# Residual sums of a decoder layer made by accumulating transfers instead of VectorE

## The chip, the cores and the metric

One core of a Trainium2 chip runs the whole kernel. The metric is the device time of one execution in microseconds, as the median of several. The core has five instruction streams: TensorE (PE), VectorE (DVE), ScalarE (ACT), GpSimd (POOL) and SyncE (SP). They run on their own and meet at semaphores. SP and POOL issue transfers, which 16 DMA engines carry out.

## The reference, cut to what matters

One layer of a hybrid decoder for 512 prompt tokens and 64 sample tokens, 2048 wide: mixer, cross-attention into a memory, squared-ReLU MLP, each behind an RMSNorm and followed by one ("sandwich"). The change touches the two places where a sub-layer's output is normalized, added to x, and x is normalized for the next sub-layer:

```python
x = x + rmsnorm(mix @ w_out, g_mix_post)
x = x + rmsnorm(cross_attn(rmsnorm(x, g_mem_pre), mem_k, mem_v, w_mem_q, w_mem_o), g_mem_post)
x = x + rmsnorm(sq_relu_mlp(rmsnorm(x, g_mlp_pre), w_up, w_down), g_mlp_post)
```

with `rmsnorm(x, g) = x * rsqrt(mean(x*x) + eps) * g` over the 2048 features. The two places are the first `+` with the norm `g_mem_pre` behind it, and the second `+` with `g_mlp_pre` behind it.

## The kernel before

Activations lie transposed: 128 features on the partitions, 16 chunks (`KC`) of features, 576 tokens along each row. `xT` is x, `yT` the sub-layer's output, both 128 x 16 x 576 float32, so one chunk is 288 KB. Matrix products keep float32 accuracy by splitting both operands in a high and a low part: three products hi*hi, hi*lo, lo*hi per tile (`parts`, line 1987, six matmuls of 288 columns for one chunk and one stripe of weights). A stripe of weights goes raw by a transfer (`w_load`, L508), high part by ScalarE (`hi`, L833 and `hi_halves`, L1028), low part by VectorE (`lo`, L1239 and `lo_halves`, L1681).

The residual stage runs twice, k = 0 behind the mixer and k = 1 behind the cross-attention. Per chunk c:

- VectorE, `residual` (L1711): `scale` multiplies yT by the row factors `n_rt` (named rstd_b in the profile, L1694; chunk 0 in halves from PSUM, L1718) and counts in `n_t`; `add` multiplies by the gain and adds into xT (L1701) and counts in `n_x`; `low` makes `act_lo` = xT * gain - act_hi (L1708) and counts in `n_lo`. The order is scale(c+2), low(c), add(c+2).
- ScalarE, `residual` (L1056): waits for `n_x`, makes `act_hi` (L1068) and the square of x in `n_sq` (L1073, named z_out), the latter only when TensorE has used the buffer (`n_used`).
- TensorE, `first_tiles` (L2365): for each chunk `col_sums` over the squares (L2353), then the six matmuls of chunk c for the first stripe. From chunk `behind` on (4 for k = 0, 6 for k = 1), each step also does chunk c - behind of the second stripe, ahead of the first stripe's. What remains of the second stripe follows, then the row factors are spread (L2361).
- SyncE: in k = 0 it waits for all 16 additions before it loads the cross-attention's caches into memory that yT holds (L594 on). In k = 1 it stores xT to HBM, four chunks at a time, each time the four are added (L618 to L621); that copy is read back near the end (L818).
- GpSimd has nothing to do in either stage.

The norm's factor for the next sub-layer isn't applied to the operands but to the product afterwards, so TensorE can start on chunk 0 before the sum over all chunks is known.

Of the kernel before, what the change touches and what calls it, by code (L numbers as in the profile page):

```python
# [14 lines left out]
F32 = mybir.dt.float32  # L15
# [148 lines left out]
def program(nc, x_prompt, x_sample, mem_prompt, state_ret, cache_k, cache_v, cache_mk, cache_mv, pages,  # L164
# [5 lines left out]
    with ctx:  # L170
# [3 lines left out]
        def sem(name):  # L174
            return ctx.enter_context(nc.semaphore(name))
# [304 lines left out]
        n_x = sem("n_x")  # L480
# [30 lines left out]
        def _(sp):  # L511
# [82 lines left out]
            sp.wait_ge(n_x, KC)  # L594
# [54 lines left out]
        def _(pool):  # L649
# [173 lines left out]
        def _(act):  # L823
# [232 lines left out]
            def residual(k, g_pre, stripe, tile):  # L1056
# [6 lines left out]
                with act.Fori(0, KC // 2) as i:  # L1063
                    for b in range(2):
                        act.wait_ge(n_x, i * 2 + (k * KC + b + 1))
                        act.sem_inc(s_idle, 1)
                        x = xT[:, bass.ds(2 * i + b, 1), :].rearrange("p a t -> p (a t)")
                        nc.scalar.activation(act_hi[:, bass.ds(2 * i + b, 1), :].rearrange("p a t -> p (a t)"), x,  # L1068
                                             ACT.Copy, scale=gT[:, bass.ds(2 * i + (g_pre + b), 1)]).then_inc(n_hi, 1)

                        act.wait_ge(n_used, i * 2 + (k * KC + b + 1))
                        act.sem_inc(s_idle, 1)
                        nc.scalar.activation(n_sq[b][:], x, ACT.Square).then_inc(n_xsq, 1)  # L1073
# [154 lines left out]
        def _(dve):  # L1228
# [1439 lines left out]
```

## Time and profile before

| | us |
|---|---|
| median of 3 runs | 3084.23 |
| lowest, highest | 3084.04, 3086.8 |
| the profiled execution | 3081.77 |
| its span | 3080.1 |
| TensorE busy | 3013.3 (98%) |
| VectorE busy | 1278.9 (42%) |
| ScalarE busy | 767.5 (25%) |
| GpSimd busy | 149.6 (5%) |
| mean granted TensorE clock | 0.992 |

"Busy" is the time in which an engine has at least one instruction under way. Times inside the profile count from the span's start. The two residual stages are short stretches of it: k = 0 from about 1211 to 1258 us, k = 1 from about 1393 to 1441 us. A timeline lists instructions with their start and duration; where one is followed by [0.69 <-DVE act_lo], its engine stood idle that long before it, until that instruction released it. Instructions overlap at their ends, so the cost of one in a row of many is the distance between starts.

### The profile page before, as it was taken

To read this page: it belongs to the slowest core of one execution; us is meant where nothing else is said; L and a number is where in the kernel's file an instruction comes from. 1 tells how busy PE (TensorE), PEld (TensorE's weight loads), DVE (VectorE), ACT (ScalarE), POOL (GpSimd) and SP (SyncE) were. 2 spreads that over 40 slices of the span, in tenths; PEclk is the share of its full clock that TensorE was granted. 3 is DMA by queue.
4 is the path that set the end of the run, shared out by engine and by line. 5 is a ranking of instruction groups with operands and counts; after the bars stand their busy time and mean duration, and the time that the engine had idled before them with its cause. 6 is when DMAs were issued, how large, how long until landed. Compare 5 with 4: busy or idle time off the path is not lost.

```text
span 3080.1 us, 48385 instructions
## 1 busy us (share of the span) xinstructions
PE 3013.3 (98%) x20106; PEld 2749.1 (89%) x20106; DVE 1278.9 (42%) x1839; ACT 767.5 (25%) x862; POOL 149.6 (5%) x254
## 2 busy tenths in 40 slices
PE   7999999999999999998999999999999999999998
PEld 6899999999899998777989889899898898998976
DVE  6544245455554445557333333323323333233235
ACT  4311123322322233434212112112121121121222
POOL 0000002312211000000000000000000000000000
PEclk8999999999999999999999999999999999999999
DMA  5433435545656453423222222222222222222242
GB/s 181 161 105 105 149 115 168 166 137 171 211 160 229 148 191 106 138 69 117 92 80 75 94 72 85 88 76 87 82 82 82 82 82 82 82 82 82 82 152 80
DMA packets 366166, 356.19 MB, mean 116 GB/s; under 512 B 9446, under 2 KB 296412, under 8 KB 363900
## 3 DMA queue, kind: packets, MB, share of 16 engines
q1 hardware_dynamic: 344696, 269.18, 28.5%
q0 software_dynamic: 21152, 85.70, 8.2%
q8 instruction: 62, 1.02, 0.1%
q14 instruction: 28, 0.23, 0.0%
q10 hardware_dynamic: 228, 0.06, 0.0%
HBM read 306.67 MB, written 48.23 MB: 115 GB/s over the span
## 4 chain that ended last, share of the span: by engine, by line
PE 91%; issue 3%; DVE 2%; DMA 2%; ACT 1%; POOL 1%; DVEq 0%; POOLq 0%; ACTq 0%
PE gemm L1987 55%; PE aux L2581 7%; PE aux L2582 7%; PE aux L2583 7%; PE gemm L2586 2%; PE gemm L2585 2%; PE aux L2093 1%; PE gemm L2070 1%; PE gemm L2016 1%; PE aux L1987 1%; DMA w_raw<-in_w_in 1%; PE aux L2133 1%; PE aux L2149 1%; DMA g_row<-in_norm_mlp_post 1%; DMA d_vp<-in_cache_diff_v 0%
## 5 line engine op out<-in xcount | busy, mean ns | idle before, releaser
L1987 PE MATMUL gemm<-act_hi,w_hi 128*128 128x288 f32 x4480 | 980.4, 300 | 6.3 <-DVE yT L1662 3.6
L1987 PE MATMUL gemm<-act_lo,w_hi 128*128 128x288 f32 x4480 | 960.2, 296 | 0.0
L1987 PE MATMUL gemm<-act_hi,w_lo 128*128 128x288 f32 x4480 | 959.8, 296 | 0.0
L1987 PEld LDWEIGHTS gemm<-act_hi,w_hi 128*128 128x128 f32 x4480 | 720.7, 189 | 37.9 <-issue 23.9
L1987 PEld LDWEIGHTS gemm<-act_hi,w_lo 128*128 128x128 f32 x4480 | 722.9, 189 | 0.0
L1987 PEld LDWEIGHTS gemm<-act_lo,w_hi 128*128 128x128 f32 x4480 | 722.8, 189 | 0.0
L1239 DVE TENSOR_TENSOR w_lo<-w_raw,w_hi 128x2048 fp32r<-128x2048 f32 x214 | 489.9, 2290 | 467.0 <-ACT w_hi L1186 325.9
L2581 PE MATMUL aux<-w_hi,u_hi 128*128 128x512 f32 x1024 | 399.7, 390 | 6.3 <-DVE w_lo L1239 6.3
L2582 PE MATMUL aux<-w_hi,u_lo 128*128 128x512 f32 x1024 | 399.0, 390 | 0.0
L2583 PE MATMUL aux<-w_lo,u_hi 128*128 128x512 f32 x1024 | 398.9, 390 | 0.0
L1186 ACT ACTIVATE w_hi<-w_raw 128x2048 fp32r<-128x2048 f32 x63 | 120.6, 1915 | 539.4 <-PE aux L2583 539.4
L833 ACT ACTIVATE w_hi<-w_raw 128x2048 fp32r<-128x2048 f32 x89 | 170.3, 1914 | 326.6 <-PE gemm L1987 256.6
L2581 PEld LDWEIGHTS aux<-w_hi,u_hi 128*128 128x128 f32 x1024 | 192.6, 188 | 49.9 <-DVE w_lo L1239 6.7
L2583 PEld LDWEIGHTS aux<-w_lo,u_hi 128*128 128x128 f32 x1024 | 192.7, 188 | 40.5
L2582 PEld LDWEIGHTS aux<-w_hi,u_lo 128*128 128x128 f32 x1024 | 192.7, 188 | 40.0
L1863 DVE SCALAR_TENSOR_TENSOR z_out<-gemm,rstd_b 128x288 f32<-128x288 f32 x126 | 51.8, 453 | 399.5 <-PE gemm L1987 397.3
L1175 ACT ACTIVATE z_out<-z_out 128x576 f32<-128x576 f32 x64 | 43.9, 686 | 603.4 <-DVE z_out L1863 603.4
L1170 ACT ACTIVATE w_hi<-w_raw 128x2048 fp32r<-128x2048 f32 x62 | 118.0, 1904 | 75.7 <-PE aux L2583 75.7
L1885 DVE TENSOR_TENSOR y_tok<-y_tok,aux 128x512 f32 x96 | 65.9, 687 | 114.2 <-PE aux L2583 114.2
L2586 PE MATMUL gemm<-w_lo,u_hi 128*64 128x512 f32 x256 | 101.4, 396 | 0.0
L2585 PE MATMUL gemm<-w_hi,u_hi 128*128 128x512 f32 x256 | 99.7, 390 | 0.0
L1868 DVE TENSOR_TENSOR u_lo<-z_out,u_hi 128x512 f32 (+1 forms) x64 | 44.3, 693 | 115.0 <-ACT u_hi L1177 115.0
(344 smaller groups left out, 2043.7 us busy)
## 6 DMA issues: line engine op xcount, KB each, us to landing
w_raw<-in_w_mlp_up SPq DMA_DIRECT2D x64, 1024.0 KB, 6.5
w_raw<-in_w_mlp_down SPq DMA_DIRECT2D x64, 1024.0 KB, 5.0
w_raw<-in_w_in SPq DMA_DIRECT2D x56, 1024.0 KB, 5.7
w_raw<-in_w_out SPq DMA_DIRECT2D x16, 1024.0 KB, 6.3
z_scratch<-z_out SPq DMA_DIRECT2D x56, 288.0 KB, 2.1
r_zin<-z_scratch POOLq DMA_DIRECT2D x8, 1152.0 KB, 6.7
d_z<-z_scratch POOLq DMA_DIRECT2D x12, 576.0 KB, 7.3
xin<-in_x_prompt POOLq DMA_DIRECT2D x6, 1024.0 KB, 6.8
```

What stands on the lines that cost most here:

```text
L833: nc.scalar.activation(w_hi[b][:], w_raw[b][:], ACT.Copy).then_inc(s_whi, 1)
L1170: nc.scalar.activation(w_hi[(b + 1) % 2][:], w_raw[(b + 1) % 2][:], ACT.Copy).then_inc(s_whi, 1)
L1186: nc.scalar.activation(w_hi[(b + 1) % 2][:], w_raw[(b + 1) % 2][:], ACT.Copy).then_inc(s_whi, 1)
L1239: V.tensor_tensor(w_lo[b][:], w_raw[b][:], w_hi[b][:].bitcast(F32), ALU.subtract).then_inc(s_wlo, 1)
L1863: ins = V.scalar_tensor_tensor(out=u_t[:, cols], in0=(G if b else bank)[2 * b + half][:, 0:TH], scalar=0.0, in1=rstd_b[:, cols], op0=ALU.m ...
L1885: ins = V.tensor_tensor(y, y, y_bank[t][:], ALU.add)
L1987: ins = M(out[half][:, 0:TH], w[b][:, cols], x[:, k, half * TH:(half + 1) * TH], start=first and n == 0, stop=last and n == 2)
L2581: M(A[t][:], hi, w_hi[b][:, cols], start=c == 0, stop=False)
L2582: M(A[t][:], lo, w_hi[b][:, cols], start=False, stop=False)
L2583: ins = M(A[t][:], hi, w_lo[b][:, cols], start=False, stop=c == FC - 1)
L2585: M(G[2][:], u_hi[:, c, TP:T + TS], w_hi[b][:, cols], start=c == 0, stop=False, skip_group_check=True)
L2586: ins = M(G[2][0:TS, :], u_hi[:, c, TP:T], w_lo[b][:, cols], start=False, stop=c == FC - 1, skip_group_check=True)
```

## The change

VectorE no longer adds. Its scaling multiplies by the row factor and by the gain in one instruction (`scalar_tensor_tensor`). GpSimd issues, for each chunk, a transfer from yT to xT that adds into the destination (`accum_op=ALU.add`), as soon as the chunk is scaled. Up to four are in flight: chunk c waits until that of chunk c - 4 has landed. Each of four semaphores `n_xd` counts the landings of every fourth chunk; they take the place of `n_x`, and `x_added` waits for them on ScalarE, VectorE and SyncE. `low(c)` runs four chunks behind the scaling instead of two. The loops over chunks on VectorE, ScalarE and SyncE are written out instead of being loops of the engine.

```diff
+        def x_added(eng, k, c):
+
+            eng.wait_ge(n_xd[c % 4], 16 * (4 * k + c // 4 + 1))
...
-            sp.wait_ge(n_x, KC)
+            for c in range(KC - 4, KC):
+                x_added(sp, 0, c)
...
-            with sp.Fori(0, KC // 4) as i:
-                sp.wait_ge(n_x, 4 * i + (KC + 4))
-                sp.sem_inc(s_idle, 1)
-                sp.dma_start(x_d[:, bass.ds(4 * i, 4), :], xT[:, bass.ds(4 * i, 4), :]).then_inc(s_spill, 16)
+            for i in range(KC // 4):
+                for c in range(4 * i, 4 * i + 4):
+                    x_added(sp, 1, c)
+                sp.dma_start(x_d[:, 4 * i:4 * i + 4, :], xT[:, 4 * i:4 * i + 4, :]).then_inc(s_spill, 16)
...
+            for k in range(2):
+                for c in range(KC):
+                    pool.wait_ge(n_t, k * KC + c + 1)
+                    if k or c >= 4:
+                        pool.wait_ge(n_xd[c % 4], 16 * (4 * k + c // 4))
+                    pool.dma_start(xT[:, c, :], yT[:, c, :], accum_op=ALU.add).then_inc(n_xd[c % 4], 16)
...
-                with act.Fori(0, KC // 2) as i:
-                    for b in range(2):
-                        act.wait_ge(n_x, i * 2 + (k * KC + b + 1))
...
+                for c in range(KC):
+                    x_added(act, k, c)
+                    nc.scalar.activation(act_hi[:, c, :], xT[:, c, :], ACT.Copy, scale=gT[:, g_pre + c:g_pre + c + 1]).then_inc(n_hi, 1)
+                    act.wait_ge(n_used, k * KC + c + 1)
+                    nc.scalar.activation(n_sq[c % 2][:], xT[:, c, :], ACT.Square).then_inc(n_xsq, 1)
...
-            def scale(c):
-                y = flat(yT[:, bass.ds(c, 1), :])
-                V.tensor_tensor(y, y, n_rt[:], ALU.mult).then_inc(n_t, 1)
-
-            def add(k, c, g_post):
-
-                at = bass.ds(c, 1)
-                x, y = flat(xT[:, at, :]), flat(yT[:, at, :])
-                dve.wait_ge(n_t, c + (k * KC + 1))
-                V.scalar_tensor_tensor(out=x, in0=y, scalar=gT[:, bass.ds(c + g_post, 1)], in1=x,
-                                       op0=ALU.mult, op1=ALU.add).then_inc(n_x, 1)
+            def scale(c, g_post):
+                y = yT[:, c, :]
+                V.scalar_tensor_tensor(out=y, in0=y, scalar=gT[:, g_post + c:g_post + c + 1], in1=n_rt[:],
+                                       op0=ALU.mult, op1=ALU.mult).then_inc(n_t, 1)
...
-                add(k, 0, g_post)
                 dve.wait_ge(n_bcs, 4 * k + 2)
-                scale(1)
-                add(k, 1, g_post)
-                with dve.Fori(0, KC - 2) as c:
-                    scale(c + 2)
+                for c in range(1, KC):
+                    scale(c, g_post)
+                    if c >= 4:
+                        low(k, c - 4, g_pre)
+                for c in range(KC - 4, KC):
                     low(k, c, g_pre)
-                    add(k, c + 2, g_post)
-                low(k, KC - 2, g_pre)
-                low(k, KC - 1, g_pre)
```

VectorE's stream at the start of the stage k = 0, before. The rows from the branch on are the loop, which runs 14 times:

```order
L1718 TENSOR_TENSOR yT<-yT,aux 128x288 [waits n_bc]
L1718 TENSOR_TENSOR yT<-yT,aux 128x288
L1701 SCALAR_TENSOR_TENSOR xT<-yT,gT,xT 128x576 [waits n_t]
L1694 TENSOR_TENSOR yT<-yT,rstd_b 128x576 [waits n_bcs]
L1701 SCALAR_TENSOR_TENSOR xT<-yT,gT,xT 128x576 [waits n_t]
L1724 UNCONDITIONAL_BRANCH
L1724 ISA
L1694 TENSOR_TENSOR yT<-yT,rstd_b 128x576
L1706 REGISTER_ALU
L1708 ISA [waits n_hi,n_x]
L1708 ISA
L1708 SCALAR_TENSOR_TENSOR act_lo<-xT,gT,act_hi 128x576
```

The same place now (line numbers of the changed kernel; n_xd0 to n_xd3 are the landing counts):

```order
L1716 SCALAR_TENSOR_TENSOR yT<-yT,gT,aux 128x288 [waits n_bc]
L1716 SCALAR_TENSOR_TENSOR yT<-yT,gT,aux 128x288
L1700 SCALAR_TENSOR_TENSOR yT<-yT,gT,rstd_b 128x576 [waits n_bcs]
L1700 SCALAR_TENSOR_TENSOR yT<-yT,gT,rstd_b 128x576 x3
L1706 SCALAR_TENSOR_TENSOR act_lo<-xT,gT,act_hi 128x576 [waits n_hi,n_xd0]
L1700 SCALAR_TENSOR_TENSOR yT<-yT,gT,rstd_b 128x576
L1706 SCALAR_TENSOR_TENSOR act_lo<-xT,gT,act_hi 128x576 [waits n_hi,n_xd1]
L1700 SCALAR_TENSOR_TENSOR yT<-yT,gT,rstd_b 128x576
```

Four scalings stand ahead of the first low part where one scaling and two additions stood, and nothing of VectorE writes xT any more.

GpSimd's stream behind its last loads of the mixer, before:

```order
L799 DMA yT<-y_scratch 128x2x576 [waits s_zst1,s_zst0,s_xt]
L799 DMA yT<-y_scratch 128x2x576 [waits s_zst1,s_zst0] x3
L818 DMA act_hi<-x_scratch 128x9216 [waits s_tile,s_spill]
L819 DMA g_row<-in_norm_mlp_post 128x2048
L170 UNCONDITIONAL_BRANCH
```

And now, cut to its first rows:

```order
L804 DMA yT<-y_scratch 128x2x576 [waits s_zst1,s_zst0,s_xt]
L804 DMA yT<-y_scratch 128x2x576 [waits s_zst1,s_zst0] x3
L826 DMA xT<-yT 128x576 [waits n_t] x4
L826 DMA xT<-yT 128x576 [waits n_xd0,n_t]
L826 DMA xT<-yT 128x576 [waits n_xd1,n_t]
L826 DMA xT<-yT 128x576 [waits n_xd2,n_t]
```

32 accumulating transfers (16 per stage) stand between the loads of yT and the load of x_scratch near the end of the kernel.

## Rows read from the trace of the kernel before

**Rows 1.** The page's list of busy us, share, instructions.

```profile
PE 3013.3 (98%) x20106; PEld 2749.1 (89%) x20106; DVE 1278.9 (42%) x1839; ACT 767.5 (25%) x862; POOL 149.6 (5%) x254
```

**Rows 2.** Chain that ended last, 1205 to 1300: start us, us, what.

```profile
1229.45 1.79 PE gemm L1987 x12
1231.62 1.78 PE gemm L1987 x12
...
1255.07 1.93 ACT w_hi L833
1257.02 2.30 DVE w_lo L1239
```

**Rows 3.** Timeline of VectorE, k = 0: start us, us, instruction, idle before.

```profile
1217.61 0.82 DVE L1701 SCALAR_TENSOR_TENSOR xT<-yT,gT,xT 128x576 f32<-128x576 f32 x1
...
1220.55 0.81 DVE L1708 SCALAR_TENSOR_TENSOR act_lo<-xT,gT,act_hi  x1
1221.28 0.81 DVE L1701 SCALAR_TENSOR_TENSOR xT<-yT,gT,xT  x1
1222.01 0.75 DVE L1694 TENSOR_TENSOR yT<-yT,rstd_b 128x576 f32 x1
1222.68 0.81 DVE L1708 SCALAR_TENSOR_TENSOR act_lo<-xT,gT,act_hi  x1
```

**Rows 4.** Timeline of VectorE, k = 1, the first addition.

```profile
1399.41 0.82 DVE L1701 SCALAR_TENSOR_TENSOR xT<-yT,gT,xT 128x576 f32<-128x576 f32 x1
```

**Rows 5.** Timeline of TensorE, k = 0: chunk 0's sums, chunks 0 to 3.

```profile
1220.26 0.71 PE L2353 MATMUL aux<-z_out,ones 128*32 128x144 f32 x8 [4.31 <-ACT z_out L1073]
1221.42 0.85 PE L1987 MATMUL gemm<-act_hi,w_hi 128*128 128x288 f32 x2 [0.46 <-DVE act_lo L1708]
...
1223.80 0.85 PE L1987 MATMUL gemm<-act_hi,w_hi 128*128 128x288 f32 x2
...
1226.17 0.85 PE L1987 MATMUL gemm<-act_hi,w_hi 128*128 128x288 f32 x2
...
1228.01 0.53 PE L1987 MATMUL gemm<-act_hi,w_hi 128*128 128x288 f32 x2
```

**Rows 6.** Stretches: length, busy us, granted clock, DMA share, GB/s.

```profile
1218.00:1222.00 4.00, 1.29 (x10) 0.81 (x11) 3.96 (x6) 3.02 (x6) 0.00 (x0) 0.50 0.96 262
1400.00:1404.00 4.00, 1.49 (x11) 1.02 (x12) 3.96 (x7) 2.82 (x5) 0.00 (x0) 0.50 0.89 244
1407.00:1409.00 2.00, 2.00 (x16) 1.14 (x15) 2.00 (x4) 1.31 (x3) 0.00 (x0) 0.72 1.01 424
953.00:957.00 4.00, 4.00 (x32) 3.44 (x31) 2.84 (x7) 2.64 (x3) 0.75 (x2) 1.00 1.08 382
```

**Rows 7.** Timeline of TensorE, k = 1: chunks 2 to 5, then sums of 6.

```profile
1407.97 0.59 PE L1987 MATMUL gemm<-act_hi,w_hi 128*128 128x288 f32 x2
...
1409.60 0.54 PE L1987 MATMUL gemm<-act_hi,w_hi 128*128 128x288 f32 x2
...
1411.73 0.53 PE L1987 MATMUL gemm<-act_hi,w_hi 128*128 128x288 f32 x2 [0.69 <-DVE act_lo L1708]
...
1413.86 0.53 PE L1987 MATMUL gemm<-act_hi,w_hi 128*128 128x288 f32 x2 [0.69 <-DVE act_lo L1708]
...
1414.85 0.45 PE L2353 MATMUL aux<-z_out,ones 128*32 128x144 f32 x8
```

**Rows 8.** Groups of instructions, the additions: busy us, mean ns, idle before.

```profile
L1701 DVE SCALAR_TENSOR_TENSOR xT<-yT,gT,xT (+1 forms) x32 | 26.3, 821 | 0.1
```

**Rows 9.** Line 788, GpSimd's four stores of 288 KB, 839.8 to 952.6.

```profile
L788 POOL DMA_DIRECT2D mix_hi_scratch<-r_yhi x4: 559/566/572, 839.8 to 952.6; - x4
...
DMA to landing us min/median/max: 3.3/3.8/4.6
```

**Rows 10.** Timeline of ScalarE, k = 0: one chunk.

```profile
1222.40 0.78 ACT L1068 ACTIVATE act_hi<-xT,gT  x1 [0.77 <-DVE xT L1701]
1223.09 0.67 ACT L1073 ACTIVATE z_out<-xT 128x576 f32 x1
```

**Rows 11.** Timeline of SyncE: cache load in k = 0, stores in k = 1.

```profile
1249.78 0.38 SPq L595 DMA_DIRECT2D c_mk<-out  x1
...
1406.26 25.87 SPq L621 DMA_DIRECT2D x_scratch<-xT  x4
```

**Rows 12.** Timeline of all engines, 1158 to 1166: GpSimd's issues and VectorE.

```profile
1160.11 2.86 POOL L799 DMA_DIRECT2D yT<-y_scratch  x4 [21.51 <-PE aux L2093]
...
1160.28 0.76 DVE L1672 TENSOR_TENSOR n_acc<-n_acc,z_out 128x576 f32<-128x576 f32 x1 [0.75 <-ACT z_out L1042]
```

More of the change, by code:

```diff
@@ L479, in program @@
         n_even = sem("n_even")
-        n_x = sem("n_x")
+        n_xd = [sem(f"n_xd{b}") for b in range(4)]
         n_xsq = sem("n_xsq")
@@ L1062, in residual @@
                 spread(n_y_bc)
-                with act.Fori(0, KC // 2) as i:
-                    for b in range(2):
-                        act.wait_ge(n_x, i * 2 + (k * KC + b + 1))
[L1066 to L1073, printed above, removed]
+                for c in range(KC):
[3 more added lines that the diff above has]
+                    nc.scalar.activation(n_sq[c % 2][:], xT[:, c, :], ACT.Square).then_inc(n_xsq, 1)
                 act.wait_ge(n_used, (k + 1) * KC + 2)
@@ L1690, in flat @@
                 return a.rearrange("p a t -> p (a t)")
-            def scale(c):
-                y = flat(yT[:, bass.ds(c, 1), :])
-                V.tensor_tensor(y, y, n_rt[:], ALU.mult).then_inc(n_t, 1)
-            def add(k, c, g_post):
-                at = bass.ds(c, 1)
-                x, y = flat(xT[:, at, :]), flat(yT[:, at, :])
-                dve.wait_ge(n_t, c + (k * KC + 1))
-                V.scalar_tensor_tensor(out=x, in0=y, scalar=gT[:, bass.ds(c + g_post, 1)], in1=x,
-                                       op0=ALU.mult, op1=ALU.add).then_inc(n_x, 1)
+            def scale(c, g_post):
+                y = yT[:, c, :]
+                V.scalar_tensor_tensor(out=y, in0=y, scalar=gT[:, g_post + c:g_post + c + 1], in1=n_rt[:],
+                                       op0=ALU.mult, op1=ALU.mult).then_inc(n_t, 1)
             def low(k, c, g_pre):
-                at = bass.ds(c, 1)
-                dve.wait_ge(n_x, c + (k * KC + 1))
+                x_added(dve, k, c)
                 dve.wait_ge(n_hi, c + (k * KC + 1))
-                V.scalar_tensor_tensor(out=flat(act_lo[:, at, :]), in0=flat(xT[:, at, :]), scalar=gT[:, bass.ds(c + g_pre, 1)],
-                                       in1=flat(act_hi[:, at, :]).bitcast(F32), op0=ALU.mult, op1=ALU.subtract).then_inc(n_lo, 1)
+                V.scalar_tensor_tensor(out=act_lo[:, c, :], in0=xT[:, c, :], scalar=gT[:, g_pre + c:g_pre + c + 1],
+                                       in1=act_hi[:, c, :].bitcast(F32), op0=ALU.mult, op1=ALU.subtract).then_inc(n_lo, 1)
             def residual(k, g_post, g_pre, stripe):
@@ L1717, in residual @@
                     y = yT[:, 0, half * TH:(half + 1) * TH]
-                    ins = V.tensor_tensor(y, y, n_y_bc[half], ALU.mult)
+                    ins = V.scalar_tensor_tensor(out=y, in0=y, scalar=gT[:, g_post:g_post + 1], in1=n_y_bc[half],
+                                                 op0=ALU.mult, op1=ALU.mult)
                 ins.then_inc(n_t, 1)
-                add(k, 0, g_post)
                 dve.wait_ge(n_bcs, 4 * k + 2)
-                scale(1)
-                add(k, 1, g_post)
-                with dve.Fori(0, KC - 2) as c:
-                    scale(c + 2)
+                for c in range(1, KC):
[3 more added lines that the diff above has]
+                for c in range(KC - 4, KC):
                     low(k, c, g_pre)
-                    add(k, c + 2, g_post)
-                low(k, KC - 2, g_pre)
-                low(k, KC - 1, g_pre)
                 recip(2 * k + 2)
```

## The prediction

> **What bounds the kernel now.** The page first: TensorE is busy 98% of the span, VectorE 42%, GpSimd 5% [rows 1]. So a change to VectorE's work can only matter where TensorE waits for it, and I looked for these places. The edited functions run twice, in the two residual stages: k = 0 (from 1217 us) and k = 1 (from 1399 us). In the chain of waits of k = 0 [rows 2] the reader sees VectorE and ScalarE only up to the first chunk; from 1229.45 it is TensorE alone, about 1.78 us of matmuls every 2.16 us, until the weights of the third stripe (ACT and DVE, 1255 to 1259).
>
> I call T the end of the scaling of chunk 0: 1217.61 in k = 0, 1399.41 in k = 1, where the first addition starts [rows 3, 4]. VectorE's period per chunk is 2.13 us (scale, low part, addition: 1220.55 to 1222.68 between low parts) [rows 3]. TensorE in k = 0 starts chunk 0 at T+3.81. Chunks 0 and 1 take 2.38 us each at the low clock (granted 0.50, the level of 1.2 GHz), the next 1.84, and chunk 4's two-chunk step begins 1.44 after that [rows 2, 5, 6]. The first two are longer than VectorE's 2.13, which puts VectorE far enough ahead for the next two, and from chunk 4 on a step has two chunks of matmuls and 2.16 us. So in k = 0 TensorE is its own bound from chunk 0 on. In k = 1 two-chunk steps start only at chunk 6; there the rows show TensorE waiting 0.69 us for act_lo twice, with steps of 2.13 where 1.37 would do (the step from 1413.86 to the matmuls of chunk 6: its col_sums at 1414.85, 0.38 of them) [rows 7]. **That is all that a faster VectorE can give back**: 0.76 twice, plus 0.2 on the step before (1.63 against 1.43), 1.7 us.
>
> **What is removed and what it gives.** 32 additions of 0.82 us, 26.3 us of VectorE time [rows 8]. The gain multiply moves into the scaling, which stays one instruction (0.75 us, at most 0.82 as a scalar_tensor_tensor) [rows 3]. VectorE's period falls to about 1.5 us, below TensorE's 2.16 and near its 1.37. Gain: 1.7 us in k = 1, nothing in k = 0. The loops are written out, which removes register work and adds instructions to fetch; both lie beside VectorE's new slack, and I cost them at nothing (a late fetch would show as a gap of VectorE or ScalarE without a releaser).
>
> **What is added: latency ahead of chunk 0.** The sum of chunk 0 took 0.82 us on VectorE. Now it is a transfer: GpSimd sees n_t, issues, 16 engines read xT and yT, add, write, and only then ScalarE may start. No transfer of the kernel before accumulates, so I bound it. The nearest rows are GpSimd's stores of one 288 KB chunk: 3.3, 3.8, 4.6 us to landing (min, median, max) [rows 9]. The max is that of the last one, issued at 952.63, and from 953 to 957 the DMA engines were at a share of 1.08 [rows 6]. That is the case here too: w_load of the next stripe moves its 1 MB in these four microseconds, share 0.96 and 0.89 [rows 6]. An accumulation reads a second operand. A plain chunk costs 0.7 us of all 16 engines (294,912 B at some 420 GB/s, read off the first x_scratch store, which moves at 1407 to 1409 [rows 6, 11]), so I add 0.7: **L = 5.3 us**, bounds 3.3 (quiet engines, the second read for nothing) and 6.0 (4.6 plus 1.4, the second read at half speed beside the load).
>
> From the landing, ScalarE starts 0.3 later (addition's end 1222.09, act_hi 1222.40), its square starts 0.69 later and takes 0.67, col_sums follows 0.13 behind and takes 0.64 before the chunk's matmuls [rows 3, 5, 10]. That is 2.43: the sums, not the low part, now come last (low part: 0.3 + 0.78 + 0.06 + 0.82 = 1.96). The four scalings that now stand before low(0) end at T+3.7, ahead of T+L, and cost nothing unless L falls below about 2.1. Chunk 0 starts at T + 5.3 + 2.43 = T+7.73, against T+3.81: **+3.9 us in each stage**, 7.8 in all. Nothing covers it: TensorE has no other matmuls in its queue there.
>
> **What is added: the rate of the transfers.** Call D the engines' time for one accumulation; I take twice a plain chunk, 1.4 us, since two operands are read; bounds 0.7 (a plain chunk) and 2.8 (as if the add took as long again as both reads; no row is nearer). The sums of chunks land at T+5.3, T+8.0 (the load still has 1.3 us of work), then every 1.4. Chunk c's col_sums can start 1.8 after its landing. In k = 0 chunk 1 is needed at T+9.5 and ready at T+9.8: +0.3; all later ones are ahead of TensorE, whose steps are 2.16. So k = 0 is **+4.2**.
> In k = 1 SyncE also stores x_scratch, 1.18 MB after every fourth chunk, 2.8 us of all engines by the same rate [rows 6, 11], now against the accumulations. Landings: T+5.3, 8.0, 9.4, 10.8, then sharing with the first store 13.0, 15.8, 18.0, 19.4, and so on up to 36.5. TensorE would want col_sums of chunk 5 at T+16.6 and can have it at 17.6, of chunk 6 at 18.9 and can have it at 19.8; from there the two go side by side (chunk 9: 26.3 wanted, 26.1 ready; chunk 15: 39.2 and 38.3). Chunk 6 started at T+15.44 before (1414.85) [rows 7], so k = 1 is 19.8 - 15.44 = **+4.4** (that is 3.9 + 0.3 + 1.9 of waits - 1.7 of gain).
> Behind the waits: GpSimd has nothing else queued (its last issues before are those at 1160.11 [rows 12], and the x_back load stands behind the MLP). VectorE's low(c-4) holds up scale(c+1), with the lead that TensorE's pace gives it. SyncE's cache loads waited for the last addition (1249.78) and are free at about T+28, earlier; its x_scratch stores are needed by ScalarE's first square of the MLP, behind all 16 chunks [rows 11]. Neither is on the path.
>
> **Sum.** 4.2 + 4.4 = +8.6 us. The profiled execution has 3081.77 us, 1.7 around its span of 3080.1: it would become 3090.4. The median of three is 2.5 us above it, 3084.23, so single runs differ by a good part of the effect; the same 8.6 us on the median give 3092.8 us.
>
> **Two rules of the Trainium skill.** A GpSimd-issued transfer needs GpSimd to write descriptors. The trace: four issues at 1160.11 took 2.86 us, 0.71 each, while VectorE ran the n_acc sum with two SBUF inputs at 1160.28 [rows 12]; nothing shows that one was held up. The Trainium skill, "SBUF — State Buffer", section "Who interferes with whom", says that a VectorE instruction with two SBUF inputs contends with GpSimd instructions that read SBUF, not with those that only write it, and that its 2-port modes lock GpSimd out of writing descriptors. By its first half nothing changes; a lock is the third rival below.
> The Trainium skill, "Collectives: The Full Stack", section "The bandwidth ceiling: the fold count and why AG ≠ RS ≠ AR", says that an add in a DMA engine costs its second read and nothing for the add, measured as 1.93 times a copy. By it D would be 0.7 x 1.93 = 1.35 (an estimate from that page), and the sum would be the same within 1 us; no row of this trace shows an add.
>
> **Rivals.** (a) *The transfers set the pace.* If D is 2.8, chunk 15 lands at about T+49 in k = 0 and, with the three stores, T+58 in k = 1, and TensorE has it 1.8 later, where it had it at T+35.1 (eleven steps of 2.16 behind chunk 4's) and T+34.9 (nine behind chunk 6's) [rows 2, 7]: +16 and +25, 3125 us. It decides from D = 1.9 (k = 0) or 1.5 (k = 1). For it: no row shows an accumulation, and k = 1 has no slack at 1.4. Against: it needs the add itself to cost time. At D = 2.1 the sum is about +18. 0.20.
> (b) *Not slower.* If the transfer finds a gap and the second read is hidden, L is 3.3: chunk 0 starts at T+5.73, +1.9 per stage, and with D under 1.2 no waits follow: 3.8 - 1.7 = +2.1, 3086.3 us. For it: small stores landed in 3.3 us. Against: the weight load is in flight at that very time in both stages. It decides below L = 5.2 where no waits follow, below about 4 with waits of my size. A little below it: TensorE finds more chunks ready when it restarts and gets its clock back sooner, worth at most 2 us per stage (two chunks at 2.38 that could take 1.37), which ends near 3082; a gain over 0.2% needs that and more. 0.24, of which 0.04 for such a gain.
> (c) *VectorE starves GpSimd.* VectorE runs without a gap from T to T+3.7; if descriptors wait for that, L is 9.0 and each stage loses 3.7 more: 8.6 + 7.4 = +16, 3100 us. The even issues at 1160.11 speak against it [rows 12]. 0.06.
> The forecast (latency in both stages, between 3088 and 3099): 0.50.
>
> **How the numbers follow.** The likeliest case gives 3092.8. The range reaches down past (b)'s 3086.3 to 3085.5 and up to 3114, which is D of about 2.5 (+30), and takes in (c); above it lies a part of (a), below it little. About 0.2%, 6 us, is what a measurement can tell from no change. Slower by more: (c), (a), and most of the forecast (from 3090.4 up): 0.06 + 0.20 + 0.38 = 0.64. Same: the rest of the forecast and most of (b): 0.12 + 0.20 = 0.32. Faster: 0.04.
>
> **What would show it.** In the profile of the changed kernel: landing of the first accumulation of each stage 5.3 us after issue (right), under 4 (b), 9 or more (c). TensorE's first chunk at T+7.7. In the timeline of k = 0, steps of 2.16 us from chunk 4 to 15; longer ones with waits for act_hi or a DMA mean (a). ScalarE's wait before act_hi should be for a DMA. The mean clock should be as now, 0.99. The stage k = 1 should no longer show steps of 2.13 at chunks 3 and 4 if landings keep up. The forecast is wrong if an accumulation costs the engines other than 1.4 us, or if chunk 0 is not late.

## The result and the profile after

| | before | after |
|---|---|---|
| median of 8 runs each, us | 3084.86 | 3094.35 |
| lowest, highest | 3082.98, 3086.8 | 3091.38, 3097.73 |
| span of the profiled execution | 3080.1 | 3092.0 |
| mean granted TensorE clock | 0.992 | 0.989 |

After to before is 1.0032, with an interval of 1.0023 to 1.0041: 9.5 us slower, where 8.6 were forecast.

The page's busy list of the changed kernel, the answer to [rows 1]: VectorE has lost 20 us of work and GpSimd has gained 27, and TensorE, the engine that counts, has not changed.

```profile
PE 3014.4 (97%) x20106; PEld 2749.9 (89%) x20106; DVE 1258.9 (41%) x1807; ACT 767.3 (25%) x862; POOL 176.3 (6%) x286
```

The timeline of the stage k = 0 after the change, all engines (start, duration, engine, instruction, idle before it and what ended that), answering to [rows 3], [rows 5] and [rows 10]:

```profile
1218.42 0.93 DVE L1716 SCALAR_TENSOR_TENSOR yT<-yT,gT,aux 128x288 f32<-128x288 f32 x2
1218.66 0.37 SPq L512 DMA_DIRECT2D w_raw<-in_w_mem_q  x1
...
1219.67 0.95 POOL L826 DMA_DIRECT2D xT<-yT  x1 [55.06 <-DVE yT L1716]
1220.13 3.00 DVE L1700 SCALAR_TENSOR_TENSOR yT<-yT,gT,rstd_b 128x576 f32<-128x576 f32 x4 [0.78 <-ACT rstd_b L1048]
1221.25 2.58 POOL L826 DMA_DIRECT2D xT<-yT  x3 [0.64 <-DVE yT L1700]
1225.28 0.78 ACT L1077 ACTIVATE act_hi<-xT,gT 128x576 fp32r<-128x576 f32 x1 [5.19 <-DMA xT<-yT]
...
1226.16 0.82 DVE L1706 SCALAR_TENSOR_TENSOR act_lo<-xT,gT,act_hi 128x576 fp32r<-128x576 f32 x1 [3.03 <-ACT act_hi L1077]
1226.69 0.78 ACT L1077 ACTIVATE act_hi<-xT,gT 128x576 fp32r<-128x576 f32 x1
...
1226.78 0.71 PE L2349 MATMUL aux<-z_out,ones 128*32 128x144 f32 x8 [9.18 <-ACT z_out L1079]
...
1227.41 0.85 PE L1983 MATMUL gemm<-act_hi,w_hi 128*128 128x288 f32 x2
```

T, the end of the scaling of chunk 0, is 1218.42 + 0.93 = 1219.35. GpSimd issues at once, and ScalarE, idle for 5.19 us until the DMA, starts act_hi at T+5.9 (before: T+1.2). Chunk 0's matmuls start at T+8.1. TensorE stood idle 9.18 us ahead of them, where it stood 4.31 before [rows 5].

The same in k = 1, where T is 1404.07 + 0.93 = 1405.00, with TensorE's three later waits for chunks 6, 10 and 15:

```profile
1404.07 0.93 DVE L1716 SCALAR_TENSOR_TENSOR yT<-yT,gT,aux 128x288 f32<-128x288 f32 x2
1404.17 0.37 SPq L512 DMA_DIRECT2D w_raw<-in_w_mlp_up  x1
...
1412.12 0.77 ACT L1077 ACTIVATE act_hi<-xT,gT 128x576 fp32r<-128x576 f32 x1 [6.38 <-DMA xT<-yT]
...
1413.61 0.71 PE L2349 MATMUL aux<-z_out,ones 128*32 128x144 f32 x8 [10.41 <-ACT z_out L1079]
...
1414.25 0.85 PE L1983 MATMUL gemm<-act_hi,w_hi 128*128 128x288 f32 x2
...
1424.87 0.45 PE L2349 MATMUL aux<-z_out,ones 128*32 128x144 f32 x8 [0.16 <-ACT z_out L1079]
...
1433.86 0.45 PE L2349 MATMUL aux<-z_out,ones 128*32 128x144 f32 x8 [0.29 <-ACT z_out L1079]
...
1445.72 0.45 PE L2349 MATMUL aux<-z_out,ones 128*32 128x144 f32 x8 [0.99 <-ACT z_out L1079]
```

The col_sums of chunk 15 are the last sign of a stage. They start at 1258.38 and 1445.72, T+39.0 and T+40.7. Before the change they started at T+35.2 and T+34.9 (T at 1217.58 and 1399.37), as these two rows of TensorE's timeline of the kernel before show:

```profile
1252.74 0.45 PE L2353 MATMUL aux<-z_out,ones 128*32 128x144 f32 x8
...
1434.27 0.45 PE L2353 MATMUL aux<-z_out,ones 128*32 128x144 f32 x8
```

So k = 0 is 3.9 us longer and k = 1 5.8 us. T itself comes 0.1 later in each stage, since the scaling of chunk 0 with the gain takes 0.93 us instead of 0.81. That makes 9.9 us, where the medians differ by 9.5; the profiled spans differ by 11.9, of which the other 2.0 lie ahead of k = 0 (1.6) and behind k = 1 (0.5), where nothing was edited.

What the DMA engines carried, in stretches of the changed kernel (length, busy us by engine, granted clock, DMA share, GB/s), beside [rows 6]:

```profile
1219.00:1225.00 6.00, 0.00 (x0) 0.00 (x0) 3.35 (x5) 0.71 (x2) 3.53 (x4) 0.50 0.95 236
1236.00:1242.00 6.00, 6.00 (x58) 4.83 (x57) 4.91 (x8) 3.72 (x6) 2.98 (x4) 1.00 1.08 187
...
1405.00:1409.00 4.00, 0.00 (x0) 0.00 (x0) 3.00 (x4) 0.71 (x2) 2.85 (x4) 0.69 0.68 175
...
1409.00:1440.00 31.00, 25.94 (x223) 20.07 (x224) 19.01 (x25) 19.03 (x28) 10.74 (x13) 0.82 1.09 262
```

From 1236 to 1242 only accumulations were under way: full engines, yet 187 GB/s, so the 294,912 B of one chunk take 1.58 us. In k = 1 the engines are full for 31 us on end. And the transfers, line 826 (issue durations in ns, then us to landing):

```profile
L826 POOL DMA_DIRECT2D xT<-yT x32: 832/848/1237, 1219.7 to 1435.2; - x32
...
DMA to landing us min/median/max: 4.2/6.3/9.1
```

### The profile page after: what moved, and what is told of

Read it like the earlier page. It is cut to its first block, busy times and chain, and to the rows that moved or that the text cites. A ratio compares the mean times of both kernels' runs of the same rounds, so it can differ in the third digit from the quotient of the medians.

```text
span 3092.0 us, 47978 instructions
## 1 busy us (share of the span) xinstructions
PE 3014.4 (97%) x20106; PEld 2749.9 (89%) x20106; DVE 1258.9 (41%) x1807; ACT 767.3 (25%) x862; POOL 176.3 (6%) x286
## 4 chain that ended last, share of the span: by engine, by line
PE 88%; issue 7%; DMA 3%; DVE 1%; POOL 1%; ACT 0%; DVEq 0%; POOLq 0%; ACTq 0%
PE gemm L1983 53%; PE aux L2577 7%; PE aux L2578 7%; PE aux L2579 7%; PE gemm L2582 2%; PE gemm L2581 2%; PE aux L2089 1%; PE gemm L2066 1%; DMA xT<-yT 1%; PE gemm L2012 1%; DMA w_raw<-in_w_in 1%; PE aux L2129 1%; PE aux L2145 1%; DMA g_row<-in_norm_mlp_post 1%; DMA d_vp<-in_cache_diff_v 0%
## 5 line engine op out<-in xcount | busy, mean ns | idle before, releaser
L1983 PEld LDWEIGHTS gemm<-act_hi,w_hi 128*128 128x128 f32 x4480 | 720.9, 189 | 35.3 <-issue 25.7
```

The source lines that it names most:

```text
L1983: ins = M(out[half][:, 0:TH], w[b][:, cols], x[:, k, half * TH:(half + 1) * TH], start=first and n == 0, stop=last and n == 2)
```

## The experiments

One table first; each experiment's reading follows. "Chunk 0" and "chunk 15" are the starts of their col_sums from T in us, k = 0 / k = 1; the next column is how much later chunk 15 is than before, both stages summed. The ratio is to the kernel before as it ran beside that kernel (medians of 3084.86 for the changed kernel, 3085.36 for e_load and e_dve4, 3085.28 for the others). Kernels with one run have no ratio.

| kernel | chunk 0 | chunk 15 | stages | median us (runs) | ratio |
|---|---|---|---|---|---|
| before | 2.7 / 2.7 | 35.2 / 34.9 | 0 | 3084.86 (8) | 1 |
| after | 7.4 / 8.6 | 39.0 / 40.7 | +9.7 | 3094.35 (8) | 1.0032 [1.0023, 1.0041] |
| e_load | 5.4 / 5.3 | 39.6 / 42.7 | +12.3 | 3099.83 (4) | 1.0049 [1.0032, 1.0066] |
| e_copy | 7.0 / 8.4 | 38.1 / 40.0 | +8.0 | 3088.39 (1) | |
| e_store | 7.3 / 8.8 | 39.4 / 37.9 | +7.3 | 3087.31 (1) | |
| e_dve4 | 2.3 / 2.3 | 36.4 / 38.5 | +4.9 | 3092.93 (8) | 1.0024 [1.0013, 1.0035] |
| e_quiet | 5.4 / 5.3 | 36.9 / 35.7 | +2.5 | 3087.68 (10) | 1.0009 [0.9999, 1.0018] |
| e_quiet4 | 2.3 / 2.3 | 36.7 / 35.5 | +2.1 | 3092.35 (10) | 1.0020 [1.0010, 1.0029] |
| e_quiet4b | 2.3 / 2.3 | 36.4 / 35.5 | +1.8 | 3087.44 (1) | |
| e_dve16 | 2.3 / 2.3 | 35.1 / 34.9 | 0.0 | 3086.55 (10) | 1.0005 [0.9996, 1.0014] |
| e_qcopy | 4.2 / 4.2 | 36.0 / 33.7 | -0.3 | 3085.78 (1) | |
| e_qsp | 4.0 / 4.0 | 35.3 / 33.2 | -1.6 | 3081.27 (1) | |

Single executions scatter by some 4 us around a median, in part outside the stages: between the last sign of k = 0 and T of k = 1 the profiled e_dve4 and e_quiet4 took 1.7 and 1.9 us longer than the kernel before (granted clocks 0.97 against 0.98), e_load 0.9, the others at most 0.2. So a single time tells little here and the stage columns more. They too are read from one execution each, and one thing moves them by chance: when the clock rises. From the col_sums of chunk 0 to those of chunk 4, TensorE took 8.28 us in k = 1 of the changed kernel, 9.39 in that of e_copy and 6.91 in that of e_store, none with a wait; in k = 0 the kernels without a wait lie between 7.35 (e_copy) and 8.34 (e_store). A difference of about 1 us in a stage is therefore no finding by itself. "Chunk 0" is free of this.

**e_load.** Is L long because of the weights? The load of the fourth stripe, which moves 1 MB beside the first accumulations, is held until chunk 3 has landed.

```diff
             for n in range(MH):
                 sp.wait_ge(s_wlo, S_MQ + n - 1)
+                if n == 3:
+                    x_added(sp, 0, 3)
                 w_load(sp, None, n % 2, mq_v[:, :, n * P:(n + 1) * P], KC)
```

(The same with `x_added(sp, 1, 3)` in the MLP's load loop.)

> The changed kernel, but SyncE's 1 MB load of the fourth stripe of weights waits until chunk 3 has been added, in both stages, so that it no longer shares the engines with the first accumulations. Theory A (the loss is the landing time of chunk 0, lengthened by this load): ScalarE starts act_hi of chunk 0 about 4.1 us after the scaling's end instead of 5.9 (k = 0) and 7.2 (k = 1), so about 5 us come back: some 4.5 us slower than the kernel before. Rival R (the transfers' rate sets the pace): the same bytes move in the same stretch, chunk 15 is no earlier, within 1 us of the changed kernel, 9.5 us slower than before. Rival G (GpSimd's own issue is slow): chunk 0 lands no earlier, 9.5 us slower.

Chunk 0 came 2.1 us earlier in k = 0 and 3.3 in k = 1: that share of L is the weights' load. But the load only moved. TensorE's waits for chunks 7 and 8 in k = 0 of e_load, which the changed kernel did not have:

```profile
1243.48 0.45 PE L2355 MATMUL aux<-z_out,ones 128*32 128x144 f32 x8 [2.02 <-ACT z_out L1085]
...
1246.13 0.45 PE L2355 MATMUL aux<-z_out,ones 128*32 128x144 f32 x8 [0.42 <-ACT z_out L1085]
```

And in k = 1 (chunk 0, then chunks 6, 7, 9 and 10):

```profile
1414.07 0.70 PE L2355 MATMUL aux<-z_out,ones 128*32 128x144 f32 x8 [7.06 <-ACT z_out L1085]
...
1425.42 0.45 PE L2355 MATMUL aux<-z_out,ones 128*32 128x144 f32 x8 [0.31 <-ACT z_out L1085]
...
1429.91 0.45 PE L2355 MATMUL aux<-z_out,ones 128*32 128x144 f32 x8 [2.26 <-ACT z_out L1085]
...
1437.40 0.45 PE L2355 MATMUL aux<-z_out,ones 128*32 128x144 f32 x8 [1.59 <-ACT z_out L1085]
...
1440.71 0.45 PE L2355 MATMUL aux<-z_out,ones 128*32 128x144 f32 x8 [1.07 <-ACT z_out L1085]
```

The landings stretched to 14.6 us at most, and both stages ended later than in the changed kernel, by 0.6 and 2.0 us. The first expectation said that 5 us come back; the rival of the rate came nearer, but the time was 14.5 us above the kernel before, not 9.5. The DMA engines' time was short as a whole, not only at the start.

**e_copy.** The transfers only copy yT over xT, so the residual sum is left out.

```diff
-                    pool.dma_start(xT[:, c, :], yT[:, c, :], accum_op=ALU.add).then_inc(n_xd[c % 4], 16)
+                    pool.dma_start(xT[:, c, :], yT[:, c, :]).then_inc(n_xd[c % 4], 16)
```

> The changed kernel, but the transfers copy yT over xT instead of adding to it: the residual sum is left out, everything else is as it was. Theory A: the second read goes, one transfer costs the engines 0.7 us instead of 1.6 to 1.7; chunk 0 lands 0.9 us earlier in each stage and the waits inside k = 1 (1.4 us) go: 6 us slower than before. Rival G (latency of an issue by GpSimd, not the adding): chunk 0 lands within 0.3 us of where it does now, 9 us slower. Rival R: if the rate were the pace, most of the loss would go, 1 to 3 us slower.

What GpSimd's queue q0 took of the engines (packets, MB, share of 16 engines over the span), first before, then after, then e_copy:

```profile
q0 software_dynamic: 21152, 85.70, 8.2%
```

```profile
q0 software_dynamic: 25760, 95.14, 9.9%
```

```profile
q0 software_dynamic: 23712, 95.14, 9.0%
```

The 32 transfers add 1.7% of 3092 us, or 1.6 to 1.7 us of all engines each; as copies 0.8% of 3085, or 0.8 each. Issuing a copy took GpSimd 0.54 us, an accumulation 0.85. Yet chunk 0 was only 0.4 and 0.2 us earlier, not the 0.9 expected: beside the load, the second read was not what made L long. No wait came behind chunk 0 in k = 1, so the waits for chunks 6, 10 and 15 need the adding. (The clock rose later here than in the changed kernel, which hides 1.1 us of the gain in k = 1.)

**e_store.** SyncE stores x only when all 16 chunks of k = 1 have landed.

```diff
             for i in range(KC // 4):
-                for c in range(4 * i, 4 * i + 4):
-                    x_added(sp, 1, c)
+                if i == 0:
+                    for c in range(KC - 4, KC):
+                        x_added(sp, 1, c)
```

> The changed kernel, but in k = 1 SyncE's four stores of x to HBM wait until all 16 chunks have been added. Theory A: chunk 0 is as late as now; the waits for chunks 6, 10 and 15 in k = 1 (1.4 us together) go, unless the stores, now all behind chunk 15, hold back ScalarE's first square of the MLP by 1 or 2 us: 8 to 10 us slower than before. Rival R (engines shared with the stores set the pace of k = 1): k = 1 loses only what k = 0 loses, 4 us: 8 us slower, with no wait for a transfer behind chunk 4.

The loss of k = 1 fell from 5.8 to 3.0 us, with chunk 0 0.2 later than it was (8.8). TensorE had no wait behind chunk 0: the waits for chunks 6, 10 and 15, 1.7 us of longer steps, need the stores as well as the adding. The other 1.4 us of the difference are the clock's. TensorE's col_sums of chunks 1 to 3 in k = 1 of e_store:

```profile
1412.74 0.71 PE L2350 MATMUL aux<-z_out,ones 128*32 128x144 f32 x8
...
1414.53 0.45 PE L2350 MATMUL aux<-z_out,ones 128*32 128x144 f32 x8
...
1415.90 0.45 PE L2350 MATMUL aux<-z_out,ones 128*32 128x144 f32 x8
```

Chunk 1 took 1.79 us and chunk 2 1.37 (granted 0.71 and 1.00), where they took 2.38 and 2.15 in the changed kernel (granted 0.50 and 0.58). The changed kernel's first store was issued at 1416.44, when its chunk 1 was already under way, and TensorE waited in neither step, so no wait behind the stores explains them. The stages' +7.3 lies below both expectations, whose lowest was 8 us.

**e_dve4.** Chunks 0 to 3 are added by VectorE, the transfers begin with chunk 4 (`BY_DVE = 4`).

```diff
-                for c in range(KC):
+                for c in range(BY_DVE, KC):
                     pool.wait_ge(n_t, k * KC + c + 1)
...
+                add(k, 0)
                 dve.wait_ge(n_bcs, 4 * k + 2)
+                lows = 0
                 for c in range(1, KC):
                     scale(c, g_post)
-                    if c >= 4:
-                        low(k, c - 4, g_pre)
+                    lag = 2 if c < BY_DVE else min(4, 2 + (c - BY_DVE) // 2 + 1)
+                    if c - lows >= lag:
+                        low(k, lows, g_pre)
+                        lows += 1
+                    if c < BY_DVE:
+                        add(k, c)
```

> The changed kernel, but chunks 0 to 3 are added by VectorE in both stages, chunks 4 to 15 by accumulating transfers. Theory A: chunk 0 is as early as in the kernel before; but the first transferred chunk, 4, is scaled only at about T+7.4, lands some 4.2 later and can be summed 1.8 after that, T+13.4, where TensorE wants it at T+11.4: the latency moves to chunk 4 and shrinks, 2 us in each stage, 4 to 5 us slower than before in all. Rival R: 12 transfers keep ahead of TensorE's pace once the start is early, no loss is left: within 1 us of before. Rival L (what is lost is only the cold start at chunk 0): also within 1 us of before, or 1.7 us faster.

TensorE's waits in k = 1 (chunks 4 and 15):

```profile
1418.65 0.45 PE L2369 MATMUL aux<-z_out,ones 128*32 128x144 f32 x8 [2.01 <-ACT z_out L1089]
...
1443.02 0.45 PE L2369 MATMUL aux<-z_out,ones 128*32 128x144 f32 x8 [0.57 <-ACT z_out L1089]
```

Chunk 0 was in time and chunk 4 late, at T+14.1 instead of T+11.2. The latency is paid where the first transferred chunk is needed, whichever it is, less the lead there; half of the loss in the stages went. The wait also cost clock: behind it the granted clock was 0.50 again (1420.4 to 1422.7), and chunk 5 took 2.38 us where 1.37 would do. Of the whole kernel's loss less is seen to go: 7.4 us over eight runs, with an interval of 4.0 to 10.8, where 4 to 5 were expected.

**e_quiet.** Both the load of the fourth stripe and the stores of x wait until all 16 chunks have landed, so that the accumulations have the DMA engines to themselves.

```diff
+                if n == 3:
+                    for c in range(KC - 4, KC):
+                        x_added(sp, 0, c)
                 w_load(sp, None, n % 2, mq_v[:, :, n * P:(n + 1) * P], KC)
```

> The changed kernel, but in both stages SyncE's load of the fourth stripe waits until all 16 chunks have been added, and in k = 1 the four stores of x follow it, so that the accumulations have the engines to themselves. Times from the start of the matmuls that spread the row factor. Theory A (what is lost is landing time: 3.6 us for a quiet accumulation, more for each other transfer that shares the engines): col_sums of chunk 0 at 8.3 as where the load was held until chunk 3; no waits for a transfer behind it; chunk 15 at 40.5 in k = 0 (before: 38.04) and 38.2 in k = 1 (before: 37.82), about 3 us slower than before in all. Rival R (one accumulation costs the engines 1.67 us and that alone sets the pace): waits remain in k = 1, chunk 15 at 42 or later there, 6 to 7 us slower. Rival D (the held load and stores are then late themselves): chunk 15 as by A, but TensorE waits for weights behind the stages, 3 us or more on top.

Line 834 of it: the fastest landing 3.4 us instead of 4.2, the slowest 6.7 instead of 9.1.

```profile
L834 POOL DMA_DIRECT2D xT<-yT x32: 834/848/1237, 1217.9 to 1425.0; - x32
...
DMA to landing us min/median/max: 3.4/5.4/6.7
```

The stages' loss fell from 9.7 to 2.5 us, about as expected. So some three quarters of it came from sharing the DMA engines: 5.4 us ahead of chunk 0, 1.7 in the waits for chunks 6, 10 and 15 (the clock's part differs by 0.1 only).

**e_quiet4 and e_quiet4b.** The last two together: VectorE adds chunks 0 to 3, and load and stores are held. The second run is the same kernel once more.

> Chunks 0 to 3 added by VectorE, 4 to 15 by accumulations, and the load and the stores held until all chunks are added. Theory A: chunk 4 is a quiet accumulation in both stages: its col_sums 1.4 us late in k = 0 (15.7, as where the load was not held, since the load is over by then) and 1.4 instead of 3.0 late in k = 1, where the store of chunks 0 to 3 no longer runs against it; steps of 1.37 for chunks 4 and 5 give 1.4 of that back: chunk 15 at 39.4 and 37.8, about 1.5 us slower than before, not to be told from it. Rival L (latency of an accumulation is the same whatever else moves): chunk 4 in k = 1 at 17.2 again, 5 us slower.

> e_quiet4 once more, for a second profile. The question is whether the 4 to 5 us that e_quiet4's profile loses behind the stage k = 1 (waits for the low part of weights, 2.2 and 7.0 us, and a clock of 0.97 there) belong to the kernel. If they do, they show again and the stages end at 39.7 and 38.5 us as before; if they are chance, the rest behind k = 1 takes about 1646 us as in the other kernels and the execution is near 3087.

The stages came near the kernel before (+2.1 and +1.8), but the whole kernel less so. Behind k = 1 TensorE waited for the low part of a stripe, where before it had not. Rows of e_quiet4b, VectorE, ScalarE and TensorE:

```profile
1446.51 0.82 DVE L1887 SCALAR_TENSOR_TENSOR z_out<-gemm,rstd_b 128x288 f32<-128x288 f32 x2 [2.22 <-ACT rstd_b L1066]
...
1451.55 0.69 ACT L1199 ACTIVATE z_out<-z_out 128x576 f32<-128x576 f32 x1 [5.08 <-issue]
...
1457.82 2.29 DVE L1263 TENSOR_TENSOR w_lo<-w_raw,w_hi 128x2048 fp32r<-128x2048 f32 x1 [0.98 <-ACT w_hi L1194]
...
1460.17 0.54 PE L2011 MATMUL gemm<-act_hi,w_hi 128*128 128x288 f32 x2 [1.66 <-DVE w_lo L1263]
```

and the stores, with four in a row from 1432.1 (tile x_scratch):

```profile
L644 SPq DMA_DIRECT2D x_scratch<-xT x4: 654/1128/1541, 1432.1 to 1435.8; - x4
...
DMA to landing us min/median/max: 9.6/12.1/15.7
```

ScalarE's first square of the MLP waits for the stores of x. Its operand was ready at 1446.51 + 0.82 = 1447.33, but ScalarE stood until 1451.55. If the slowest store is the last issued, it landed at 1435.8 + 15.7 = 1451.5, just then. In e_quiet the same sum gives 1433.2 + 16.6 = 1449.8, and there the square started at 1449.83. In the kernel before it started 0.04 us behind its operand. What stands behind the square on ScalarE, the high part of the next stripe among it, came late, and then the low part and TensorE. So stores and load held together cost TensorE 1.7 us behind the stage here (2.2 in e_quiet4, 0.9 in e_quiet; none in e_store, where the load wasn't held and the stores landed within 10.2 us). The profiled span of e_quiet4 was 6.2 us above that of e_quiet4b, 3.1 of them behind k = 1, which e_quiet4b did not have. But its time, 3087.44, is not the usual one: of the ten runs of this kernel nine took 3089.91 us or more. Stages, T and this wait make some 4 us; the ratio over ten runs says 6.2, with an interval of 3.1 to 8.9, where 1.5 were expected. What makes up the rest, if it is real, stays open.

**e_dve16.** No transfers at all: VectorE adds, with the gain already in the scaling and the loops written out (`BY_DVE = 16`).

> No transfers: all 16 chunks are added by VectorE, with the written-out loops and the gain in the scaling as in the changed kernel, and the low part two chunks behind. Theory A: these two cost nothing: chunk 15 at 38.0 and 37.8 from the spreading, as before, within 1 us of before. Rival F (instruction fetch for the longer code, or the slower scaling): steps of VectorE's period over 2.13 us, gaps without a releaser, 1 to 4 us slower than before.

The stages end as before, within 0.1 us, and the time can't be told from before. Neither the written-out loops nor the fused scaling cost anything or give anything. In the stages all of the loss is the transfers'.

**e_qsp.** e_quiet, but SyncE issues plain copies in place of GpSimd's accumulations; the residual sum is left out.

```diff
+                    for c in range(KC):
+                        sp.wait_ge(n_t, 0 * KC + c + 1)
+                        if 0 or c >= 4:
+                            sp.wait_ge(n_xd[c % 4], 16 * (4 * 0 + c // 4))
+                        sp.dma_start(xT[:, c, :], yT[:, c, :]).then_inc(n_xd[c % 4], 16)
```

> As the kernel with load and stores held, but each transfer is a plain copy of yT over xT issued by SyncE (the residual sum is left out; these cannot add). Theory A: a quiet SyncE transfer of 288 KB to HBM landed in 2.1 us in the kernel before; here col_sums of chunk 0 start at about 7.0 from the spreading (8.3 for GpSimd's quiet accumulation, 5.56 for VectorE's addition), 1.4 late, so even a fast issue without the second read doesn't reach VectorE; chunk 15 at 39.4 in k = 0 and 37 in k = 1. Rival G (nearly all of the latency is GpSimd's issue): chunk 0 at 6 or less.

Chunk 0 came 1.3 us late and chunk 15 of k = 1 at T+33.2, 1.7 us ahead of before. So 3.0 us were regained between them: 1.7 in the steps of chunks 3, 4 and 5 (1.39, 1.37 and 1.38 us where they took 1.58, 2.12 and 2.13), which is the gain that the prediction gave a faster VectorE; 0.6 because chunk 0's low part no longer came last; and 0.8 because the clock rose earlier (chunks 1 and 2).

**e_qcopy.** e_quiet with plain copies by GpSimd, the residual sum left out: it differs from e_quiet by the adding alone, from e_qsp by the issuer alone.

> As e_quiet (the load of the fourth stripe of weights and SyncE's stores of x held until all 16 chunks have landed), but GpSimd's transfers only copy yT over xT, so the residual sum is left out; it differs from e_quiet only in the adding, and from e_qsp only in the issuer. If the second read and the add cost latency of their own when the DMA engines are quiet, chunk 0's col_sums starts clearly ahead of e_quiet's 8.4 us after the spreading of the row factors; if GpSimd's way of issuing is what costs, it starts at 8.4 too and not at e_qsp's 7.0. My theory (engines' time 0.8 us less per transfer, issue 0.3 less): 7.5 (7.2 to 7.9) in both stages, chunk 15 at 37 in k = 1, VectorE's gain there complete. Rival (issuer alone): 8.3, chunk 15 at 38. Time within 3 us of e_quiet either way.

ScalarE's first act_hi in k = 0, e_qcopy (T = 1220.18) and then e_qsp (T = 1218.20):

```profile
1222.88 0.78 ACT L1085 ACTIVATE act_hi<-xT,gT 128x576 fp32r<-128x576 f32 x1 [1.96 <-DMA xT<-yT]
```

```profile
1220.73 0.78 ACT L1089 ACTIVATE act_hi<-xT,gT 128x576 fp32r<-128x576 f32 x1 [1.78 <-DMA xT<-yT]
```

T+2.7 and T+2.5, against T+3.9 in e_quiet. The issuer costs 0.2 us and the adding 1.2. The expectation put chunk 0's col_sums 7.5 us behind the spreading of the row factors, and they came 7.5 and 7.2 behind it.

## Why the prediction held, and where it was off

**The mechanism** was the forecast one: TensorE bound but for the start of each stage, the latency of the first transfer ahead of it with nothing to cover it, steps of 2.16 us from chunk 4 on in k = 0. The forecast of +8.6 met +9.9 in the stages and +9.5 in the median. That it came so close is in part luck: chunk 0 was later than forecast by 0.3 and 1.5 us, the forecast waits right behind it (0.3 in k = 0, 2.2 in k = 1) all but failed to come, and others came that it did not have. Now the terms.

**L, the landing of the first accumulation, 5.3 us**, was the term that mattered most and was mis-sized. ScalarE started act_hi at T+5.9 and T+7.1; less the 0.3 between landing and start, L was 5.6 and 6.8, the second above the stated bound of 6.0. The prediction counted L from T, though GpSimd issued only 0.3 us later (1219.67 and 1405.29); from the issue on it was 5.3 in k = 0, as forecast, and 6.5 in k = 1. The runs take it apart. From an act_hi at T+1.2 by VectorE, k = 0 / k = 1:

| part | us | from |
|---|---|---|
| a transfer instead of VectorE | 1.3 / 1.3 | e_qsp - before |
| issued by GpSimd, not SyncE | 0.2 / 0.2 | e_qcopy - e_qsp |
| the adding | 1.2 / 1.1 | e_quiet - e_qcopy |
| the weight load beside it | 2.0 / 3.3 | after - e_quiet |

The prediction took 3.8 to 4.6 for a transfer beside a load and 0.7 for the second read. With quiet engines the landing takes 3.5 and the adding 1.1 of it; it is the load that was priced too low, at 1.3 in the whole (4.6 less 3.3). The parts hold in this order of taking away: beside the load, leaving out the adding gave only 0.4 and 0.2 (e_copy). Why it costs 1.3 us more in k = 1 isn't shown: the load was issued 0.69 us ahead of T in k = 0, 0.83 in k = 1, and the engines' share behind T was lower (0.68 from 1405 to 1409).

**L to the matmuls, 2.43 us**: 0.3 + 1.5 to col_sums + 0.6 to the matmuls, as the prediction had it. The sums came last, the low part with them. The four scalings ended at T+3.8, and VectorE then idled 3.03 us: no cost, as said.

**k = 0, +4.2**: +3.9. Chunk 0's matmuls were 4.2 late instead of 3.9. The 0.3 us wait for chunk 1 did not come, since chunk 0 was itself later and chunk 1 had landed by then (its act_hi at 1226.69 has no wait). TensorE took 0.35 back over chunk 2, where the clock rose sooner.

**k = 1, +4.4**: +5.8. The prediction put chunk 6 at T+19.8, and it stood at T+19.9 (1424.87). Here errors cancel: chunk 0 was 1.5 us later than thought, the waits of 2.2 us behind it shrank to 0.16, because a later TensorE finds more chunks landed, and chunk 2 ran at a granted clock of 0.58 and took 0.5 us longer than before. From chunk 6 on the two were to run side by side; instead TensorE waited for chunks 10 and 15, in all 1.4 us of longer steps (2.51 and 3.22 for 2.16). This is the term that failed in k = 1. In sum: 5.4 us at chunk 0, 1.5 of gain, 0.5 of clock and 1.4 of waits make the 5.8.

**D, 1.4 us** of the engines for an accumulation, measured 1.58 (stretch 1236 to 1242) to 1.7 (queue shares), while a copy takes 0.8. At 2.16 us a chunk this leaves k = 0 free, as forecast. In k = 1 with the 1.18 MB stores the prediction itself gave 1.5 as the point from which the rate decides. It was passed a little, and so the rival (a) did a little: 1.4 us, not 25. Both the adding and the stores are needed for it (no such wait in e_copy or e_store). The Trainium skill, "Collectives: The Full Stack", section "The bandwidth ceiling: the fold count and why AG ≠ RS ≠ AR", has an add in the DMA engines at 1.93 times a copy; these runs show 1.6 to 1.7 against 0.8, about twice, so the trace agrees.

**The gain of 1.7 us** from a faster VectorE is real: e_qsp and e_store have all of it in the steps of chunks 3 to 5. The changed kernel has 1.5 of it (1.37, 1.37 and 1.61 where the steps were 1.58, 2.12 and 2.13); the wait for chunk 6 took the rest. It does not show in the stage's end, since the later rise of the clock and the waits for chunks 10 and 15 took more than it gave.

**GpSimd's issue** took 0.85 us instead of the 0.71 of [rows 12]. Rival (c) fell: three issues were done 2.58 us after the first began, 0.86 each, two of the three while VectorE ran without a gap (until 1408.78), and a single one took 0.85 while VectorE idled (1412.63), as these rows of the changed kernel show:

```profile
1405.78 3.00 DVE L1700 SCALAR_TENSOR_TENSOR yT<-yT,gT,rstd_b 128x576 f32<-128x576 f32 x4 [0.78 <-ACT rstd_b L1048]
...
1407.00 2.58 POOL L826 DMA_DIRECT2D xT<-yT  x3 [0.86 <-DVE yT L1700]
...
1412.63 0.85 POOL L826 DMA_DIRECT2D xT<-yT  x1 [3.05 <-DMA xT<-yT]
...
1413.00 0.82 DVE L1706 SCALAR_TENSOR_TENSOR act_lo<-xT,gT,act_hi 128x576 fp32r<-128x576 f32 x1 [4.22 <-ACT act_hi L1077]
```

The lock of which the Trainium skill speaks ("SBUF — State Buffer", section "Who interferes with whom") shows in none of these rows.

**Rival (b)**, not slower, needed L below about 4. e_quiet has such an L (3.5), its stages lose 2.5 us where (b) said 2.1, and its ratio is 1.0009 with an interval that holds 1: so (b) was worked out rightly, and it was the load and the stores beside the transfers that kept it from coming true. No variant that still adds beats the kernel before, and little was to be had: its steps at chunks 3 to 5 were 1.7 us longer for VectorE's additions, 0.05% of the time.

## What to carry to other kernels

Before moving work from an engine with slack to transfers, find the first consumer of each stage: the transfer's latency is paid there once per stage, and here VectorE's saved 20 us bought at most 1.7. Price that latency with what is in flight at the same moment, from rows of just such a moment; holding the other transfer back for a few chunks only moved the collision here (e_load), and holding it to the end made a later consumer wait (e_quiet). An accumulating transfer cost the DMA engines about twice a copy here (1.6 to 1.7 us against 0.8), so count it against every store and load of its stretch, and not over the kernel's mean.

## What was not expected of the hardware

- An accumulation within SBUF of 288 KB takes 16 engines 1.6 to 1.7 us, a copy 0.8, and GpSimd 0.85 us to issue instead of 0.54.
- A 1 MB load issued 0.7 to 0.8 us ahead of such a transfer made its landing 2.0 us later in one stage and 3.3 in the other.
- The clock rises at another chunk from execution to execution. Chunks 0 and 1 of k = 0 took 2.38 us each at granted 0.50, as before, but chunk 2 took 1.49 instead of 1.84 [rows 5]; this is the 0.35 us that k = 0 took back. It does not follow the idle time ahead: after 8.3 us of idle in k = 0, TensorE took 7.35 us to chunk 4 in e_copy and 8.34 in e_store, and in k = 1 9.39 us after 9.4 of idle (e_copy) and 6.91 after 10.6 (e_store). Why isn't shown. The rows (timeline of TensorE of the changed kernel, k = 0, chunks 2 to 4):

```profile
1232.17 0.65 PE L1983 MATMUL gemm<-act_hi,w_hi 128*128 128x288 f32 x2
...
1233.66 0.53 PE L1983 MATMUL gemm<-act_hi,w_hi 128*128 128x288 f32 x2
...
1235.04 0.53 PE L1983 MATMUL gemm<-act_hi,w_hi 128*128 128x288 f32 x2
```
